# First query chunk of the experts with tokens stationary, a one-operation shift and scale in the norm, and regrouped argument operations of the gated heads

## The reference, cut to what matters

```python
h = rms_norm(x, g_norm1) * (1 + scale1) + shift1
proj = h @ w_in            # q, k, v of 8 stick-breaking heads; q, k, v, o, i, f of 4 gated heads
# gated heads (mlstm), chunk-wise there, over the whole causal square in the kernel:
log_d = where(causal, a[t] - a[s] + i[s], -inf);  m = running maximum
s_qk = (q @ k.T) * exp(log_d - m);  h_ml = (s_qk @ v) / max(abs(sum(s_qk)), exp(-m))
x = x + gate1 * (concat(y_sb, y_ml) @ w_out)
h2 = rms_norm(x, g_norm2) * (1 + scale2) + shift2
q = h2 @ w_q_peer          # 1024 -> 2048: 8 heads x 2 halves x 128
scores = einsum('bshpc,hpnc->bshpn', q, sub_keys)   # 16 x 128 scores per token
# top 16 of each half, top 16 of the sums, softmax; then, for the chosen experts of 16384:
y = sum_k gate_k * gelu(h2 @ u_k) * v_k;  x = x + gate2 * y
```

## Time and profile before

| | |
|---|---|
| time, median of 3 runs | 1453.67 us (1452.08 to 1457.14) |
| the profiled execution | 1455.23 us, its span 1453.9 us |
| mean granted TensorE clock | 0.965 |
| busy: PE / DVE / ACT / POOL | 95% / 67% / 43% / 2% |
| DMA | 317 MB, 218 GB/s |

### The profile page before, as it was taken

One profiled execution on the slowest core, in us unless ns is written; L12 is line 12 of the kernel. 1 busy time (PEld: TensorE's weight loads), 2 busy tenths in 40 slices (PEclk: granted clock), 3 DMA queues, 4 the chain that ended last, 5 costly groups with the idle time before them and its releaser, 6 DMA issues.

```text
span 1453.9 us, 19658 instructions
## 1 busy us (share of the span) xinstructions
PE 1386.2 (95%) x8262; PEld 1234.5 (85%) x8262; DVE 966.9 (67%) x1527; ACT 623.3 (43%) x534; POOL 35.1 (2%) x31
## 2 busy tenths in 40 slices
PE   6897968999999999799999999999999999999998
PEld 5786747888888887599999999999998888888886
DVE  5443645888846584747887869999546566666664
ACT  5333434434323854435344434444444444444441
POOL 0010010000002000000000000000000000000000
PEclk9898979999988998899999999999999999999999
DMA  7440316899724221344777656978898777777760
GB/s 304 149 174 1 116 55 263 314 371 382 293 95 188 87 88 59 145 160 167 249 230 231 226 189 217 276 241 247 254 357 294 282 271 301 299 269 303 296 261 29
DMA packets 83239, 317.39 MB, mean 218 GB/s; under 512 B 6096, under 2 KB 40144, under 8 KB 53200
## 3 DMA queue, kind: packets, MB, share of 16 engines
q1 hardware_dynamic: 83152, 316.14, 60.3%
HBM read 281.51 MB, written 34.60 MB: 217 GB/s over the span
## 4 chain that ended last, share of the span: by engine, by line
PE 93%; DVE 3%; ACT 2%; issue 1%; DMA 0%; POOL 0%; ACTq 0%; POOLq 0%
PE psum L412 91%; PE psum L415 2%; DVE slab_lo L1352 1%; ACT slab_hi L992 0%; DVE residual L1418 0%; ACT arena L995 0%; ACT x_hi L1006 0%; DMA arena<-in_mem 0%; DVE arena L1391 0%; DVE arena L1389 0%; ACT arena L1083 0%; POOL statistics L406 0%; DVE arena L1387 0%; DVE arena L1415 0%; DVE arena L1371 0%
## 5 line engine op out<-in xcount | busy, mean ns | idle before, releaser
L1352 DVE TENSOR_TENSOR slab_lo<-slab_raw,slab_hi 128x2048 fp32r<-128x2048 f32 x207 | 472.5, 2292 | 260.1 <-ACT slab_hi L992 250.6
L992 ACT ACTIVATE slab_hi<-slab_raw 128x2048 fp32r<-128x2048 f32 x207 | 394.0, 1911 | 355.1 <-PE psum L412 355.1
L412 PE MATMUL psum<-x_hi,slab_hi 128*128 128x256 f32 x1216 | 348.2, 286 | 3.6 <-ACT x_hi L1006 2.7
L412 PE MATMUL psum<-x_hi,slab_lo 128*128 128x256 f32 x1216 | 344.9, 284 | 0.0
L412 PE MATMUL psum<-x_lo,slab_hi 128*128 128x256 f32 x1216 | 344.9, 284 | 0.0
L412 PE MATMUL psum<-slab_hi,x_hi 128*128 128x512 f32 x768 | 309.8, 403 | 17.6 <-ACT x_hi L1006 8.2
L412 PE MATMUL psum<-slab_lo,x_hi 128*128 128x512 f32 x768 | 305.4, 398 | 0.0
L412 PE MATMUL psum<-slab_hi,x_lo 128*128 128x512 f32 x768 | 305.4, 398 | 0.0
L412 PEld LDWEIGHTS psum<-x_hi,slab_hi 128*128 128x128 f32 x1216 | 234.0, 192 | 4.8 <-issue 3.1
L412 PEld LDWEIGHTS psum<-x_lo,slab_hi 128*128 128x128 f32 x1216 | 234.2, 193 | 0.0
L412 PEld LDWEIGHTS psum<-x_hi,slab_lo 128*128 128x128 f32 x1216 | 233.9, 192 | 0.0
(11 more groups left out here) (233 smaller groups left out, 1244.0 us busy)
## 6 DMA issues: line engine op xcount, KB each, us to landing
slab_raw<-in_ex_u SPq DMA_DIRECT2D x64, 1024.0 KB, 5.9
slab_raw<-in_ex_v SPq DMA_DIRECT2D x64, 1024.0 KB, 4.9
arena<-in_w_ada SPq DMA_DIRECT2D x24, 1024.0 KB, 6.4
slab_raw<-in_w_in SPq DMA_DIRECT2D x22, 1024.0 KB, 5.5
slab_raw<-in_w_gu SPq DMA_DIRECT2D x22, 1024.0 KB, 6.8
hidden_store<-arena SPq DMA_DIRECT2D x32, 512.0 KB, 6.8
gates_store<-arena SPq DMA_DIRECT2D x8, 2048.0 KB, 9.7
arena<-hidden_store SPq DMA_DIRECT2D x32, 512.0 KB, 5.7
```

The lines of the kernel that those rows point to most:

```text
L412: return PE.matmul(out, lhsT, rhs, start=start, stop=stop)
L992: ACTE.activation(slab_hi[:, slot, :], raw[:, slot, :], ACT.Copy).then_inc(hi_made[slot], 1)
L1352: DVE.tensor_tensor(slab_lo[:, slot, :], raw[:, slot, :], slab_hi[:, slot, :].bitcast(f32), ALU.subtract).then_inc(lo_made[slot], 1)
```

## The change

In the experts' first chunk the queries are made with tokens stationary by normed_chunk (as in other norms): transposes of token half 0, 12 products, transposes of half 1, 36 products, into banks 4 and 5. ScalarE copies the result as query_rows (a new tile in the arena), TensorE transposes it back in eight tiles between the two halves of chunk 1, and query_out(0) then copies from banks 0 and 1 as before. ScalarE's order of slab_hi moves: that of S_PQ stands ahead of mix_out and that of S_PQ+1 ahead of the gate copy; those of S_PQ+4 and S_PQ+5 lie on the two sides of query_out(0). In x_full with a shift, four tensor_scalar operations (one per tile, multiply and add with two columns) replace the two operations over four tiles. The gated heads' 24 argument operations are put in the order: eight early spreads, the first half of slab S_IN2+12's products, eight late spreads, eight masks, the second half of the products.

```diff
--- before.py
+++ after.py
@@ -271,6 +271,7 @@
         R_SK, R_SC, R_QT = 0, 2048, 14336
         sk, scores = carve(R_SK, PEER_H * 2, NKEYS), carve(R_SC, TB, 2 * PEER_H, NKEYS)
         qT3 = [carve(R_QT + 1024 * n, 4, S) for n in range(2)]
+        query_rows = carve(12288, TB, 512)
         U = lambda x: x.bitcast(u32)
         tv, ti, tf = (carve(6144 + 512 * n, TB, 2 * PEER_H, TOPK) for n in range(3))
         bv, bp = carve(7680, TB, PEER_H, TOPK), carve(7936, TB, PEER_H, TOPK)
@@ -807,18 +808,24 @@
             ins.then_inc(sem("ml_max_transposed"), 1)
             PE.wait_ge(*after("sb_arg_opened", SB_H // 2))
             PE.wait_ge(*after("ml_rows_negated", 1))
+            early = lambda hh: ps[:, hh // 2, (hh % 2) * S:(hh % 2) * S + S]
+            late = lambda hh: ps[:, 2, hh * P:hh * P + P]
+            head = lambda hh, n: ident[0:ML_H, hh:hh + 1].to_broadcast([ML_H, n])
             for hh in range(ML_H):
-                head = ident[0:ML_H, hh:hh + 1]
-                for o, s0, t0 in ((ps[:, hh // 2, (hh % 2) * S:(hh % 2) * S + S], 0, 0),
-                                  (ps[:, 2, hh * P:hh * P + P], P, P)):
-                    mm(o, er[:, s0:s0 + P], head.to_broadcast([ML_H, S - t0]), True, False)
-                    mm(o, head.to_broadcast([ML_H, P]), cm[:, t0:S], False, False)
-                    ins = mm(o[:, 0:P], ident[:], c2["ml_mask"], False, True)
-            ins.then_inc(sem("ml_arg_made"), 1)
+                mm(early(hh), er[:, 0:P], head(hh, S), hh % 2 == 0, False)
+                mm(early(hh), head(hh, P), cm, False, False)
             PE.wait_ge(*after("ml_v_copied", 1))
             take(S_IN2 + 12)
-            for tb in range(TB):
-                half_products(6, S_IN2 + 12, 0, tb)
+            half_products(6, S_IN2 + 12, 0, 0)
+            for hh in range(ML_H):
+                mm(late(hh), er[:, P:S], head(hh, P), hh == 0, False)
+                mm(late(hh), head(hh, P), cm[:, P:S], False, False)
+            for hh in range(ML_H):
+                mm(early(hh)[:, 0:P], ident[:], c2["ml_mask"], False, hh % 2 == 1)
+            for hh in range(ML_H):
+                ins = mm(late(hh), ident[:], c2["ml_mask"], False, hh == ML_H - 1)
+            ins.then_inc(sem("ml_arg_made"), 1)
+            half_products(6, S_IN2 + 12, 0, 1)
             PE.wait_ge(*after("ml_max_copied", 1))
             PE.wait_ge(*after("conv_made", 1))
             for hh in range(ML_H):
@@ -881,9 +888,6 @@
                     ins.then_inc(sem("first_rows_made"), 1)
 
 
-            for tb in range(TB):
-                x_transposes(PEER, 0, tb)
-
             def feature_half(bank, n, half):
                 bh, bl = parts(n % NSLOT, 4, 512)
                 take(n)
@@ -900,12 +904,17 @@
                 if c >= 2:
                     PE.wait_ge(*after("query_copied", c - 1))
                 for half in range(2):
-                    if c == 0:
-                        x_ready(PEER, 1, half)
                     feature_half(2 * (c % 2), S_PQ + 2 * c + half, half)
-
+                    if c == 1 and half == 0:
+                        PE.wait_ge(*after("query_rows_copied", 1))
+                        for m in range(4):
+                            for tb in range(TB):
+                                ins = tr(ps[:, m // 2, (m % 2) * S + tb * P:(m % 2) * S + tb * P + P],
+                                         query_rows[:, tb, m * P:m * P + P])
+                        ins.then_inc(sem("query_transposed"), 1)
+
+            normed_chunk(4, S_PQ, PEER, 0)
             PE.wait_ge(*after("sub_keys_loaded", 16))
-            queries(0)
             for c in range(4):
                 if c < 3:
                     queries(c + 1)
@@ -1249,11 +1258,11 @@
             ACTE.activation(oml, oml, ACT.Exp, scale=-1.0).then_inc(sem("ml_o_made"), 1)
             ACTE.wait_ge(*after("ml_y_made", 1))
             ACTE.activation(mlsq, yml, ACT.Square).then_inc(sem("ml_y_squared"), 1)
-            hi(S_OUT2 + 3)
+            hi(S_OUT2 + 3, S_PQ)
             mix_out(xh, 0, 2)
+            hi(S_PQ + 1)
             ACTE.wait_ge(*after("gate1_spread", 1))
             ACTE.activation(g1, banks(2, 2), ACT.Copy).then_inc(sem("gate1_made"), 1)
-            hi(S_PQ, S_PQ + 1)
 
 
             for tb in range(TB):
@@ -1262,7 +1271,10 @@
                 x_hi(PEER, tb)
 
             def query_out(c):
-                slab_done(ACTE, S_PQ + 2 * c + 1)
+                if c == 0:
+                    ACTE.wait_ge(*after("query_transposed", 1))
+                else:
+                    slab_done(ACTE, S_PQ + 2 * c + 1)
                 if c >= 2:
                     ACTE.wait_ge(*after("keys_scored", c - 1))
                 ACTE.activation(qT3[c % 2], banks(2 * (c % 2), 2).rearrange("p (k n) -> p k n", k=4),
@@ -1276,8 +1288,11 @@
                     sem("scores_copied"), 1)
 
             hi(S_PQ + 2, S_PQ + 3)
+            slab_done(ACTE, S_PQ + 1)
+            ACTE.activation(query_rows, ps[:, 4:6, :], ACT.Copy).then_inc(sem("query_rows_copied"), 1)
+            hi(S_PQ + 4)
             query_out(0)
-            hi(S_PQ + 4, S_PQ + 5)
+            hi(S_PQ + 5)
             query_out(1)
             scores_out(0)
             hi(S_PQ + 6, S_PQ + 7)
@@ -1386,9 +1401,11 @@
                 if shift is None:
                     DVE.tensor_tensor(full, src, of(gain), ALU.mult).then_inc(sem("x_full"), 1)
                 else:
-                    V(DVE.tensor_tensor(full, src, of(gain), ALU.mult))
-                    V.after()
-                    DVE.tensor_tensor(full, full, of(shift), ALU.add).then_inc(sem("x_full"), 1)
+                    for k in range(4):
+                        kk = 4 * half + k
+                        ins = DVE.tensor_scalar(full[:, k], src[:, k], gain[:, kk:kk + 1], shift[:, kk:kk + 1], ALU.mult,
+                                                ALU.add)
+                    ins.then_inc(sem("x_full"), 1)
 
             def x_split(norm, bank, tb, gain, shift=None):
                 for half in range(2):
```

## The result

The changed kernel took 1439.74 us, median of 6 runs (1439.49 to 1446.06), beside 1453.55 for the kernel before (1452.08 to 1457.14): ratio 0.9919, 95% interval 0.9901 to 0.9937. That is 13.8 us by the medians and 9 to 14 by the interval; forecast were 8.5. The profiled execution took 1439.54 us, its span 1438.2, at a mean granted clock of 0.975 (0.965 before).

What follows compares the result with a forecast made beforehand. TensorE's products, 91% of the chain, were taken as the bound, so only its waits, half clock or other instructions mattered. 5.6 + 0.5 + 2.4 = 8.5 us off 1455.23 gave 1446.7, forecast 1445.0 on the median's scale; range 1440.5 to 1450.5.

Steps and rivals of the forecast that it cites:

- Part 1: Experts' first chunk: query products restart 6.9 us earlier after the norm, 1.3 given back, worth 5.6 us.
- Rival 3: Products broken into dozens by transposes or 4-row work never bring the clock back: slower, 1460.8 us; chance 0.06.
- Part 2: x_full with one operation per tile, 0.26 us each: 0.5 us gained at block 2's second norm, range 0 to 0.6.
- the upper bound, 0.33: New x_full: highest duration per tile considered, 0.33 us, meaning no gain, and a loss beyond it.
- Part 3: Gated heads' 24 arguments regrouped around products: 19.3 us to the qk products against 21.65, worth 2.4 us.
- the products between the blocks: Between early and late arguments, 12 products should bring the clock back: some 10 us at half clock instead of 13.5.
- Rival 1: Regrouped arguments gain nothing because the clock falls add up to the same half-clock time: 1447.6 us; chance 0.13.
- half clock up to the last slab product: Worst end for the arguments: half clock from 547.5 through the slab products, a loss given as 2.7 us.
- rival 2: VectorE's choice of experts sets the pace, so the earlier start only lengthens TensorE's waits: 1453.5 us; chance 0.11.
- the best cases: Experts' first chunk gaining 7 us and the arguments 5 us, giving 1441 us.
- 7.3 as its end: Best end for the regrouped arguments, if the clock does not fall at all: 7.3 us gained.

Runs made afterwards that it cites:

- the run without the move: Whole change, but with ScalarE's two slab_hi of the first query slabs behind the gate copy as before: 1445.65 us, ratio 0.9949 against the kernel before.
- part 3 alone: Kernel before with only the new order of the gated heads' argument operations: 1447.74 us, ratio 0.9967 against the kernel before.

## Why the prediction was right and where it was off

The forecast, faster by 8.5 us, had the direction and the mechanism. Against the means of three executions each:

**Part 1** held. The restart was to come 6.9 us earlier and 1.3 were to be given back; measured are 6.6 (23.65 to 17.06) and 1.2 (217.2 to 218.4): 5.4 for 5.6. Each step of it is on record: L1415 free of slab_lo (1.2 by the run without the move, forecast 1.5 and 1.2 for its two places), no wait of 0.3 us or more at the second token half, and 5.9 us from the last output product's end to the first query product, forecast 5.5. (The 12.9 that the prediction sets beside it counts from that product's start; from its end it was 12.5.) The clock was back within the dozen in two executions; in the third the whole dozen ran at half clock, 5.46 us from 596.86, and the clock was back with the transposes behind it; the 219.15 of its queries includes this. Rival 3, a clock that never returns in broken-up products, is refuted by 601.00:605.00 at 1.00.

**Part 2**: the step that failed is the duration per tile, 0.26 from the nearest row; it is 0.33. That row reads from SBUF and is the last term of a chain of its own kind; the upper bound, 0.33, had been written down and was right. Of the 0.5 us at the second norm 0.1 came, the wait of 0.33 that is now 0.22, and in part 1 the 0.35 counted in is the difference of 6.9 to 6.6.

**Part 3** was sized too low: 2.4 us, measured 5.3 to 5.9 by the stretches up to the qk products. Two terms failed. The 4-row operations were costed at their old distances of 0.52 and 0.32; in a group they take 0.43 and 0.22, since part of the old distance was the change from one kind of operation to another. I had used this argument for the masks (0.41 to 0.23) and not for the operations beside them. With it the sum is 14.3 - 8 x 0.09 - 8 x 0.10 = 12.8 instead of 14.3; measured are 12.9, the 18.0 us from the first argument less half of the 10.2 at half clock. And around the arguments the half-clock time fell from 13.7 or 17.1 us to 6.8 or 10.2, where 13.5 to 10 had been assumed. The 10.2 of the first profile is as forecast, but ahead of the arguments, where the prediction had no term, 3.4 us less fell than in the kernel before. From the hidden layer's transposes to the qk products the kernel before spent 34.1, 37.6 and 34.1 us at half clock, the changed one 27.3 three times, so 3.4 to 5.1 us came by the clock, for 1.75 forecast. The expected benefit of the products between the blocks, the forecast's reason for fewer falls, does not exist: grouped without them is as fast. Rival 1, arguments that gain nothing, is refuted by the run with part 3 alone. (A slip beside it: with half clock up to the last slab product the loss would be 14.3 + 10.3 less 21.65, 2.9 and not 2.7; nothing hangs on it.)

**Later**: rival 2, that VectorE gives it back, did not occur: the rest took 622.7 in both. In one execution of three the waits for the gates, unchanged at 2.1 us in all, were followed by a stretch at half clock that cost 1.4.

**The time itself**, 1439.74, lies 0.8 below the range, and below the 1441 of the best cases that were added up. Those took 5 us for part 3, though the prediction had named 7.3 as its end; 5.3 to 5.9 came. Part 3's 3 us too little explain the place below the range, and part 2's missing 0.4 and the 1.4 at half clock behind the gates in one execution of three took a little of it back. The start could have moved it by as much: the clock's places there span 5 us from one execution to the next, and the text had left out this spread. The sum was made against one profiled execution whose start was the slowest of the three.

## What to carry to other kernels

Group small operations by kind on TensorE before asking what stands between the groups: the distance between two starts read in a mixed order includes the switch, and the grouped price must be read from a row with the same operation among its like. Where a stage waits for a norm, make the first token half enough to start it, and look at what stands ahead of the norm's first step on each engine's list. Before a difference between two profiles is explained, cut both at the same instructions and take a second execution of each: here 4.8 of 15.7 us lay in a start where nothing had been changed.

## What the runs showed of the hardware that was not expected

- Four tensor_scalar operations of 128x128 from PSUM with two column operands take 1.29 us, as long as two operations of 128x512 with the wait between them (1.31).
- From the start of one 4-row fp32 product of 256 columns to the next start are 0.43 us within a group of them and 0.52 to 0.54 where it is the first after another kind or the last ahead of one; of 128 columns 0.22 and 0.32.
- With 4-row work in groups of two between products the granted clock stayed at 1.00 from 541 to 566; in groups of eight or more, and in the old order with masks between, it fell to 0.50.
- The same instructions, from the start to the hidden layer's transposes, took 411.9, 412.6 and 417.1 us in three executions of one kernel, with the 0.50 stretches at unequal places.
